# Filter layers spaced over more steps, the filter's output as split products, two norms' columns by transposes

## Chip, cores and metric

One core of a Trainium2 chip runs the kernel. The metric is the device time of one execution in microseconds (us). Engines: PE (TensorE matmul), DVE (VectorE), ACT (ScalarE), POOL (GpSimd, here mostly a queue of DMAs) and SP (the queue of the weight stream).

## What is computed

A backbone of two layers over 256 latent tokens of width 1024 (fp32), with 256 context tokens in layer 0:

```
for layer i in 0, 1:
  x = x + 0.5 * gate2 * rms(ffn(norm(x, shift0, scale1)))          # FFN 0 / FFN 2, ctx too in layer 0
  y = attention + short conv (layer 0)  |  Hyena long conv (layer 1)
  x = x + gate5 * rms(y)
  x = x + 0.5 * gate8 * rms(ffn(norm(x, shift6, scale7)))          # FFN 1 / FFN 3
norm(x, sh, sc) = rms(x) * g * (1 + sc) + sh
(gate, shift, scale)_b = (silu(c) @ w_mod[i] + b_mod[i])[b]        # nine blocks of 1024 per layer
filter: z (256 x 33); three times h = sin(freq * (h @ w + b)), width 64;
        filt = (h @ w4) (256 x 2048) * window; its spectrum is used by the long convolution of layer 1
```

## The kernel before

**Products.** fp32 operands are split into a high part (rounded to fp32r) and a low part (the rest): a product is three fp32r matmuls, high by high, high by low, low by high (L1671 to L1673, L1732 to L1734). The weights come as 350 units of 128 x 1024 through a ring of six buffers (SP, L463). A unit's high part is made on ACT (L617) and its low part on DVE (L1006), four units ahead of PE. Some small products are plain fp32 matmuls.

**The FFNs.** FFN 1 (second of layer 0), 2 and 3 run eleven turns of six steps; step (i, k) is turn i, unit k: steps 0 to 3 are gate and up columns (24 matmuls of 256 columns each), steps 4 and 5 the down product (12 matmuls of 512 each). Every engine has the same list of turns, and `peeled=at_steps(places, calls)` hangs further calls on steps of it; these places are written by hand for PE, ACT and DVE apart. There is no scheduler: each engine executes its list in order and waits on semaphores.

**Modulation jobs.** A job (layer, block, half, stream) is a product of c with 1024 x 512 of `w_mod`: POOL loads it in four chunks of 0.5 MB (`load_job`, L515) as DVE frees them, DVE makes eight multiply-adds (L1021, L1023) and a split (L1033), ACT the rounding (L694), PE two sums over the rows (`job_sum`, at the next turn's step 0). `JOBS` lists them by FFN, one for each turn; `JOB_0`, `JOB_L` are the first numbers. For gates (blocks 2, 5, 8) PE sums into `mean_p` and DVE makes the gate (`gate_out`, L1043 and L1045) in a tile that POOL filled with the bias (`load_gate`), times the gain of the norm in `z_tok` (`load_gain`, slot by `GATE_SLOT`). The other blocks' sums are gathered in `job_p`; after the last of a batch ACT copies them (`batch_rows`), PE turns them into columns (`batch_columns`) and DVE adds the bias (`batch_out`, `norm_coef`).

**The filter** runs beside FFN 1, at the steps `FILTER_AT`: three calls of `filter_layer` (PE, fp32, L2079, bank `mean_p`), each followed on DVE by `sine_argument` (seven dependent operations) and on ACT by `sine`, then four of `filter_out` (PE, fp32, L2089, banks `job_p` and `mean_p`), each followed on DVE by `filter_sums`. Weights, window and transform matrices come by POOL before FFN 1 (`filt_in`, L582 to L589).

**Norms 3 and 5** (`IN_PAIRS`: the latent and the context stream before the mixer of layer 0) have their transposed, scaled x made beside weight products: DVE makes a diagonal matrix of 1/rms (`spread`, L1114) and PE multiplies blocks of x by it (`norm_columns`, L1721), after the ninth context unit's down product (norm 3; its last two blocks after the thirteenth) and after the ninth unit of the input projection (norm 5). DVE and ACT then apply scale and shift.

**The opening of an FFN.** When the normed input is complete (`h_ready`) POOL orders the gate and gain loads of the coming gates, and after them the further chunks of jobs; at the same time SP's ring refills.

Of the kernel before, what the change touches and what calls it, by code (L numbers as in the profile page):

```python
# [22 lines left out]
F32 = mybir.dt.float32  # L23
# [52 lines left out]
        [(1, b, h, LAT) for b in (1, 3, 4, 2) for h in range(2)],  # L76
        [(1, b, h, LAT) for b in (6, 7, 5) for h in range(2)],
        [(1, 8, h, LAT) for h in range(2)]]
JOB_0 = [0, 22, 30, 36]
JOB_L = [AHEAD, 20, 28, 34]  # L80
# [10 lines left out]
GATE_SLOT = [0, 1, 0, 0, 0, 0]  # L91
# [111 lines left out]
def program(nc, wstream, wmod, cvec_in, bmod, gate_rows, small, x_in, ctx_in, rpb, mask_in, ident_in, turn_in, zfeat, fw1, fw2,  # L203
            fw3, fw4, fcols, window_in, dft_in, out):
    with ExitStack() as ctx:
# [115 lines left out]
        w4 = k_re[:, :, :].rearrange("p a b -> p (a b)")  # L321
        window = k_s
# [128 lines left out]
        odd_out = sem("odd_out")  # L451
        inv_done, inv_step = sem("inv_done"), sem("inv_step")
# [48 lines left out]
        def _(pool):  # L501
# [86 lines left out]
            pool.dma_start(w4[0:HY_FFN, :], fw4).then_inc(filt_in, 16)  # L588
            pool.dma_start(window, window_in).then_inc(filt_in, 16)  # L589
            pool.wait_ge(h_ready, 8 * 5)  # L590
            load_gate(1, 2)
            load_gain(1, 2)
# [3 lines left out]
            load_gate(1, 5)  # L596
            load_gain(1, 5)
# [12 lines left out]
        def _(a):  # L610
# [319 lines left out]

            def spectrum_out(i):
# [20 lines left out]
            ffn(1, peeled=at_steps([(6, 2)] + FILTER_AT, [lambda: batch_rows(1)] + [lambda l=l: sine(l) for l in range(3)]))  # L952
# [47 lines left out]
        def _(v):  # L1000
# [109 lines left out]
            def spread(q, t):  # L1110

                i = 2 * q + t
                reciprocal(q, t)
                nc.vector.tensor_scalar(diag[:, t, :], ident[:, :], rstd[:, i:i + 1], None, ALU.mult).then_inc(diag_done, 1)  # L1114
# [431 lines left out]
            def sine_argument(l):  # L1546

                if l == 0:
                    v.wait_ge(filt_in, 16 * 7)
# [12 lines left out]
                assert count[0] == FD_SIN[l]  # L1562

# [18 lines left out]
            ffn(1, peeled=at_steps([(7, 0)] + FILTER_AT, [lambda: (batch_out(1), norm_coef(9), norm_coef(11))]  # L1582
# [85 lines left out]
        def _(pe):  # L1668
# [45 lines left out]
            def norm_columns(q, t, kts=range(KT)):  # L1714
# [3 lines left out]
                for kt in kts:  # L1718
                    if q == 1 and t == 0 and kt % 2 == 0:
                        pe.wait_ge(xt_copied, kt // 2 + 1)  # L1720
                    ins = nc.tensor.matmul(columns_of(q, kt)[:, t * P:(t + 1) * P],  # L1721
                                           X[NORMS[q][2]][:, t, kt * P:(kt + 1) * P], diag[:, t, :], start=True, stop=True)
# [192 lines left out]
            for ft in range(FT):  # L1915
# [5 lines left out]
                if ft == 8:  # L1921
# [17 lines left out]
            for idx in range(16):  # L1939
# [8 lines left out]
                if idx == 8:  # L1948
                    norm_columns(5, 0)
                    norm_columns(5, 1)  # L1950
# [120 lines left out]
            def filter_layer(l):  # L2071
                if l == 0:
                    pe.wait_ge(filt_in, 16 * 7)
                    pe.wait_ge(gate_free, 10)
# [6 lines left out]
            def filter_out(i):  # L2081
                th, half = i % 2, i // 2
                if i == 0:
                    pe.wait_ge(fa, 3)
# [3 lines left out]
                for b, bank in enumerate((job_p, mean_p)):  # L2088
                    ins = nc.tensor.matmul(bank[:, :], hid[H, th * P:(th + 1) * P],  # L2089
# [261 lines left out]
```

## Time and profile before

| | us |
|---|---|
| median of 3 runs | 1338.75 (1336.57 to 1341.46) |
| profiled execution, its own time | 1343.3 |
| span of its profile | 1341.5 |
| PE busy | 1306.6 (97%) |
| DVE, ACT busy | 982.1 (73%), 632.9 (47%) |
| mean granted clock of PE | 0.992 of full |

The span is what the trace covers; the execution's own time has 1.8 us around it. Busy time of PE counts overlapping matmuls as modelled, so it shows where PE works, not how well; the start times of neighbouring matmuls tell the pace. A time in brackets in a timeline is the idle time before an instruction, with the one that released it.

### The profile page before, as it was taken

Reading aid. Unit: us, or ns where it says so; the run is one execution under the profiler, and the core shown is the slowest. Engines: PE = TensorE matmul, PEld = TensorE weight load, DVE = VectorE, ACT = ScalarE, POOL = GpSimd, SP = SyncE. Lnnn points to the kernel's source line nnn. Section 1 sums busy time; section 2 is a strip of 40 time slices with the busy share of each in tenths; the row PEclk is TensorE's granted clock in tenths of the full one; section 3 lists DMA queues with packets and bytes.
Section 4 is the critical chain, followed back from the end, with each engine's and each line's share of the span. In section 5 each row is a group of like instructions: output and inputs, shape, how many; then the busy total and the mean of one; then the engine's idle time right before and its main releaser. Section 6 shows DMA issues by size and latency. Waiting matters only on the chain.

```text
span 1341.5 us, 21469 instructions
## 1 busy us (share of the span) xinstructions
PE 1306.6 (97%) x7794; PEld 1125.8 (84%) x7794; DVE 982.1 (73%) x1447; ACT 632.9 (47%) x969; POOL 118.1 (9%) x209
## 2 busy tenths in 40 slices
PE   6899999999999999999999999999999999999997
PEld 3678777887778988789999868999998987989996
DVE  5788777788776776759888778887558797865554
ACT  6632333332376665755444337444447434644443
POOL 3000010111000422011111000110000000000000
PEclk8999999999999999999999989999999999999999
DMA  9555566777655753259888635886653536656652
GB/s 361 186 171 178 199 203 248 254 244 262 227 173 173 204 147 105 79 174 363 292 303 296 198 118 198 309 299 198 189 188 127 158 110 204 236 173 188 183 185 102
DMA packets 76359, 275.12 MB, mean 205 GB/s; under 512 B 9226, under 2 KB 9781, under 8 KB 75712
## 3 DMA queue, kind: packets, MB, share of 16 engines
q1 hardware_dynamic: 52128, 187.00, 42.4%
q0 software_dynamic: 24160, 87.12, 19.0%
q8 instruction: 50, 0.82, 0.2%
q14 instruction: 21, 0.17, 0.0%
HBM read 273.04 MB, written 1.05 MB: 204 GB/s over the span
## 4 chain that ended last, share of the span: by engine, by line
PE 86%; DVE 7%; ACT 3%; DMA 2%; issue 1%; DVEq 0%; SPq 0%; ACTq 0%
PE gu L1671 16%; PE gu L1673 16%; PE gu L1672 16%; PE acc L1732 8%; PE acc L1734 8%; PE acc L1733 8%; DVE wlo_r L1006 2%; PE acc L1721 2%; DMA wlo<-in_wstream_dram 1%; ACT whi L617 1%; PE acc L2017 1%; PE acc L2028 1%; DMA x_lat<-in_x_in_dram 1%; PE acc L1995 1%; PE acc L1996 1%
## 5 line engine op out<-in xcount | busy, mean ns | idle before, releaser
L1671 PE MATMUL gu<-h_hi,whi 128*128 128x256 f32 (+1 forms) x1688 | 518.0, 307 | 4.2 <-DVE h_lo L1131 1.3
L1672 PE MATMUL gu<-h_lo,whi 128*128 128x256 f32 (+1 forms) x1688 | 515.3, 305 | 0.0
L1673 PE MATMUL gu<-h_hi,wlo_r 128*128 128x256 f32 (+1 forms) x1688 | 515.0, 305 | 0.0
L1006 DVE TENSOR_TENSOR wlo_r<-wlo,whi 128x1024 fp32r<-128x1024 f32 x350 | 421.5, 1222 | 100.9 <-ACT whi L617 99.3
L617 ACT ACTIVATE whi<-wlo 128x1024 fp32r<-128x1024 f32 x350 | 360.3, 1049 | 97.8 <-DMA wlo<-in_wstream_dram 97.5
L1671 PEld LDWEIGHTS gu<-h_hi,whi 128*128 128x128 f32 x1688 | 318.8, 189 | 28.6 <-issue 4.0
L1672 PEld LDWEIGHTS gu<-h_lo,whi 128*128 128x128 f32 x1688 | 318.8, 189 | 19.0 <-issue 0.7
L1673 PEld LDWEIGHTS gu<-h_hi,wlo_r 128*128 128x128 f32 x1688 | 319.4, 189 | 15.5
L1023 DVE SCALAR_TENSOR_TENSOR part<-wm,cvec,part 128x512 f32<-128x512 f32 x266 | 199.5, 750 | 6.7
L1732 PE MATMUL acc<-whi,act_hi 128*128 128x512 f32 x440 | 176.7, 402 | 2.5 <-DVE act_lo L1219 2.0
L1734 PE MATMUL acc<-wlo_r,act_hi 128*128 128x512 f32 x440 | 174.9, 397 | 0.0
L1733 PE MATMUL acc<-whi,act_lo 128*128 128x512 f32 x440 | 174.5, 397 | 0.0
L515 POOL DMA_DIRECT2D wm<-in_wmod_dram x128 | 67.6, 529 | 734.0 <-DVE part L1023 459.1
L1732 PEld LDWEIGHTS acc<-whi,act_hi 128*128 128x128 f32 x440 | 83.2, 189 | 27.3 <-DVE act_lo L1219 3.9
L1734 PEld LDWEIGHTS acc<-wlo_r,act_hi 128*128 128x128 f32 x440 | 83.1, 189 | 20.0
L697 ACT ACTIVATE gated<-gu 128x256 f32<-128x256 f32 x66 | 25.3, 383 | 156.2 <-PE gu L1673 156.2
L1733 PEld LDWEIGHTS acc<-whi,act_lo 128*128 128x128 f32 x440 | 83.3, 189 | 17.8
L1214 DVE TENSOR_TENSOR act<-gated,gu 128x256 f32<-128x256 f32 x66 | 27.7, 420 | 80.2 <-ACT gated L697 79.9
L694 ACT ACTIVATE total_hi<-part 128x512 fp32r<-128x512 f32 x38 | 24.0, 631 | 78.6 <-DVE part L1023 78.6
L751 ACT ACTIVATE act_hi<-act 128x256 fp32r<-128x256 f32 x22 | 9.2, 419 | 103.6 <-DVE act L1304 103.6
L1219 DVE TENSOR_TENSOR act_lo<-act,act_hi 128x256 fp32r<-128x256 f32 x88 | 37.2, 423 | 20.4 <-ACT act_hi L701 16.4
L701 ACT ACTIVATE act_hi<-act 128x256 fp32r<-128x256 f32 x66 | 27.6, 418 | 44.2 <-DVE act L1214 44.2
(337 smaller groups left out, 1233.2 us busy)
## 6 DMA issues: line engine op xcount, KB each, us to landing
wlo<-in_wstream_dram SPq DMA_DIRECT2D x350, 512.0 KB, 3.6
wm<-in_wmod_dram POOLq DMA_DIRECT2D x132, 512.0 KB, 6.1
area<-in_wmod_dram POOLq DMA_DIRECT2D x11, 512.0 KB, 19.6
z<-in_gate_rows_dram POOLq DMA_DIRECT2D x6, 512.0 KB, 6.7
gate_keep<-in_gate_rows_dram POOLq DMA_DIRECT2D x5, 512.0 KB, 7.1
area<-in_rpb_dram POOLq DMA_DIRECT2D x32, 64.0 KB, 3.6
x_lat<-in_x_in_dram SPq DMA_DIRECT2D x1, 1024.0 KB, 7.5
area<-in_ctx_in_dram SPq DMA_DIRECT2D x1, 1024.0 KB, 8.8
```

The source lines that it names most:

```text
L515: pool.dma_start(wm[:, 2 * part_:2 * part_ + 2, :], src[:, 2 * part_:2 * part_ + 2, :]).then_inc(wm_landed[part_ // 2], 16)
L617: nc.scalar.activation(whi[:, phase % RING, :], raw[:, phase % RING, :], ACT.Copy).then_inc(hi_done, 1)
L1006: nc.vector.tensor_tensor(wlo[:, u.base % RING, :], raw[:, u.base % RING, :], whi[:, u.base % RING, :].bitcast(F32), ALU.subtract).then_in ...
L1023: ins = nc.vector.scalar_tensor_tensor(out=part[:, :], in0=wm[:, kt, :], scalar=c, in1=part[:, :], op0=ALU.mult, op1=ALU.add)
L1214: nc.vector.tensor_tensor(dst, gated[:, s, :], gu[:, s, T:2 * T], ALU.mult).then_inc(act_mul, 1)
L1219: nc.vector.tensor_tensor(act_lo[:, s, :], act[:, s, :], act_hi[:, s, :].bitcast(F32), ALU.subtract).then_inc(act_lo_done, 1)
L1671: nc.tensor.matmul(out_, w_hi, x_hi, start=start, stop=False, skip_group_check=True)
L1672: nc.tensor.matmul(out_, w_hi, x_lo, start=False, stop=False, skip_group_check=True)
L1673: return nc.tensor.matmul(out_, w_lo, x_hi, start=False, stop=stop, skip_group_check=True)
L1732: nc.tensor.matmul(y, x_hi[:, tok], whi[:, s, cols], start=kt_first, stop=False, skip_group_check=True)
L1733: nc.tensor.matmul(y, x_lo[:, tok], whi[:, s, cols], start=False, stop=False, skip_group_check=True)
L1734: ins = nc.tensor.matmul(y, x_hi[:, tok], wlo[:, s, cols], start=False, stop=kt_last, skip_group_check=True)
```

## The change

The two jobs of gate (1, 2) move from FFN 1 to FFN 2, the filter's calls take new steps, `w4` is loaded twice (rows 0 to 63 and 64 to 127) and rounded into `spare`, hid is put as high over low parts on 128 rows, so that one matmul of 128 rows makes hid_hi w_hi + hid_lo w_hi and a second of 64 rows adds hid_hi w_lo. For norms 3 and 5, DVE scales x itself into `spare` and PE transposes it. Norm 3's and norm 5's columns come one unit later. POOL no longer waits for `h_ready` ahead of FFN 1's jobs.

```diff
--- before.py
+++ after.py
@@ -73,11 +73,11 @@
 
 JOBS = [[(0, b, h, s) for b in (2, 3, 4) for h in range(2) for s in (LAT, CTX)]
         + [(l, b, h, LAT) for l, b in ((0, 5), (0, 8), (0, 6), (0, 7), (1, 0)) for h in range(2)],
-        [(1, b, h, LAT) for b in (1, 3, 4, 2) for h in range(2)],
-        [(1, b, h, LAT) for b in (6, 7, 5) for h in range(2)],
+        [(1, b, h, LAT) for b in (1, 3, 4) for h in range(2)],
+        [(1, b, h, LAT) for b in (6, 7, 2, 5) for h in range(2)],
         [(1, 8, h, LAT) for h in range(2)]]
-JOB_0 = [0, 22, 30, 36]
-JOB_L = [AHEAD, 20, 28, 34]
+JOB_0 = [0, 22, 28, 36]
+JOB_L = [AHEAD, 20, 26, 34]
 AHEAD_CHUNKS = 4 * AHEAD
 CHUNK_SLOT = [2, 3, 4, 5, 2, 3, 4, 5, 2, 3, None, 4, 5, None, 4, 5]
 AHEAD_LOADS = [(1, 0), (0, 0), (1, 1), (0, 1)]
@@ -88,7 +88,7 @@
 GATE_NORM = {2: 1, 5: 3, 8: 5}
 GATE_RES = {2: 0.5, 5: 1.0, 8: 0.5}
 GATE_JOBS = [job for jobs in JOBS for job in jobs if job[1] in GATE_NORM]
-GATE_SLOT = [0, 1, 0, 0, 0, 0]
+GATE_SLOT = [0, 1, 0, 0, 1, 0]
 
 
 COLS_AHEAD = [(0, b, h, s) for b, h in AHEAD_LOADS for s in (LAT, CTX)]
@@ -319,6 +319,10 @@
         p_f = y_f[:, 0:2, :]
         m_f = y_f[:, 2:4, :]
         w4 = k_re[:, :, :].rearrange("p a b -> p (a b)")
+        w4_lo = area_r[:, 0:2 * D]
+        w4_hi = spare_r[:, :, :].rearrange("p a b -> p (a b)")
+        hid_at = 10 * D + 7 * T
+        hid_both = area_r[:, hid_at:hid_at + T]
         window = k_s
         u_t = z
         u_f = spare[:, :, :].rearrange("p w (s n) -> p w s n", s=2)
@@ -449,6 +453,7 @@
         fp, fa, fd = sem("filter_pe"), sem("filter_act"), sem("filter_dve")
         tr_done, un_out, uf_done, yf_step = sem("tr_done"), sem("un_out"), sem("uf_done"), sem("yf_step")
         odd_out = sem("odd_out")
+        out_hi, out_lo = sem("out_hi"), sem("out_lo")
         inv_done, inv_step = sem("inv_done"), sem("inv_step")
         stored = sem("stored")
 
@@ -585,16 +590,15 @@
             pool.dma_start(fw[0:HY_FFN, 128:192], fw3).then_inc(filt_in, 16)
             pool.dma_start(fc[0:HY_FFN, :], fcols).then_inc(filt_in, 16)
             pool.dma_start(dft, dft_in).then_inc(dft_landed, 16)
-            pool.dma_start(w4[0:HY_FFN, :], fw4).then_inc(filt_in, 16)
+            for rows_ in (slice(0, HY_FFN), slice(HY_FFN, 2 * HY_FFN)):
+                pool.dma_start(w4[rows_, :], fw4).then_inc(filt_in, 16)
             pool.dma_start(window, window_in).then_inc(filt_in, 16)
-            pool.wait_ge(h_ready, 8 * 5)
-            load_gate(1, 2)
-            load_gain(1, 2)
             with pool.Fori(JOB_L[1] + 1, JOB_L[2] + 1) as l:
                 load_job(l, gemv, steps_before(l))
             pool.wait_ge(h_ready, 8 * 6)
-            load_gate(1, 5)
-            load_gain(1, 5)
+            for b in (2, 5):
+                load_gate(1, b)
+                load_gain(1, b)
             with pool.Fori(JOB_L[2] + 1, JOB_L[3]) as l:
                 load_job(l, gemv, steps_before(l))
 
@@ -928,6 +932,13 @@
                 a.wait_ge(fd, FD_SIN[l])
                 nc.scalar.activation(hid[0:HY_FFN, :], sin_r[0:HY_FFN, :], ACT.Sin).then_inc(fa, 1)
 
+            def output_his():
+                a.wait_ge(filt_in, 16 * 8)
+                for c in range(2):
+                    nc.scalar.activation(w4_hi[:, c * D:(c + 1) * D], w4[:, c * D:(c + 1) * D], ACT.Copy).then_inc(out_hi, 1)
+                a.wait_ge(fa, 3)
+                nc.scalar.activation(hid_both[0:HY_FFN, :], hid[0:HY_FFN, :], ACT.Copy).then_inc(out_hi, 1)
+
             def spectrum_out(i):
 
                 half, what, w = SPECTRUM[i]
@@ -949,7 +960,8 @@
                 spectrum_out(i + 2)
                 spectrum_out(i + 3)
 
-            ffn(1, peeled=at_steps([(6, 2)] + FILTER_AT, [lambda: batch_rows(1)] + [lambda l=l: sine(l) for l in range(3)]))
+            ffn(1, peeled=at_steps([(6, 4)] + SINE_AT + [(7, 5)], [lambda: batch_rows(1)]
+                                   + [lambda l=l: sine(l) for l in range(3)] + [output_his]))
             load_table(ACT.Sqrt)
             spectra_norms(8, U_FFN[2] + 2, 0)
             load_table(ACT.Silu)
@@ -1111,6 +1123,10 @@
 
                 i = 2 * q + t
                 reciprocal(q, t)
+                if q in IN_PAIRS:
+                    nc.vector.tensor_scalar(spare[:, t, :], X[NORMS[q][2]][:, t, :], rstd[:, i:i + 1], None,
+                                            ALU.mult).then_inc(diag_done, 1)
+                    return
                 nc.vector.tensor_scalar(diag[:, t, :], ident[:, :], rstd[:, i:i + 1], None, ALU.mult).then_inc(diag_done, 1)
 
             def scale_columns(q, kt):
@@ -1546,7 +1562,7 @@
             def sine_argument(l):
 
                 if l == 0:
-                    v.wait_ge(filt_in, 16 * 7)
+                    v.wait_ge(filt_in, 16 * 8)
                 v.wait_ge(fp, l + 1)
                 step(nc.vector.tensor_scalar(sin_a[H, :], mean_p[H, 0:T], fc[H, l:l + 1], fc[H, 3:4], ALU.add, ALU.mult))
                 settle()
@@ -1561,6 +1577,16 @@
                 step(nc.vector.tensor_scalar(sin_r[H, :], sin_a[H, :], PI_F, -PI_F, ALU.min, ALU.max))
                 assert count[0] == FD_SIN[l]
 
+            def output_los():
+                v.wait_ge(fa, 3)
+                for c in range(2):
+                    v.wait_ge(out_hi, c + 1)
+                    nc.vector.tensor_tensor(w4_lo[H, c * D:(c + 1) * D], w4[H, c * D:(c + 1) * D],
+                                            w4_hi[H, c * D:(c + 1) * D].bitcast(F32), ALU.subtract).then_inc(out_lo, 1)
+                v.wait_ge(out_hi, 3)
+                nc.vector.tensor_tensor(hid_both[HY_FFN:2 * HY_FFN, :], hid[H, :], hid_both[H, :].bitcast(F32),
+                                        ALU.subtract).then_inc(out_lo, 1)
+
             def filter_sums(i):
 
                 th, half = i % 2, i // 2
@@ -1579,7 +1605,7 @@
                                                     in1=p_f[:, th, cols], op0=ALU.mult, op1=ALU.add))
                 assert count[0] == FD_SUM[i]
 
-            ffn(1, peeled=at_steps([(7, 0)] + FILTER_AT, [lambda: (batch_out(1), norm_coef(9), norm_coef(11))]
+            ffn(1, peeled=at_steps([(7, 4), (8, 0)] + FILTER_AT, [lambda: (batch_out(1), norm_coef(9), norm_coef(11)), output_los]
                                    + [lambda l=l: sine_argument(l) for l in range(3)]
                                    + [lambda i=i: filter_sums(i) for i in range(4)]))
             norms(8, (U_FFN[2] + 2, U_FFN[2] + 3))
@@ -1718,8 +1744,12 @@
                 for kt in kts:
                     if q == 1 and t == 0 and kt % 2 == 0:
                         pe.wait_ge(xt_copied, kt // 2 + 1)
-                    ins = nc.tensor.matmul(columns_of(q, kt)[:, t * P:(t + 1) * P],
-                                           X[NORMS[q][2]][:, t, kt * P:(kt + 1) * P], diag[:, t, :], start=True, stop=True)
+                    if q in IN_PAIRS:
+                        ins = nc.tensor.transpose(columns_of(q, kt)[:, t * P:(t + 1) * P], spare[:, t, kt * P:(kt + 1) * P],
+                                                  ident[:, :])
+                    else:
+                        ins = nc.tensor.matmul(columns_of(q, kt)[:, t * P:(t + 1) * P],
+                                               X[NORMS[q][2]][:, t, kt * P:(kt + 1) * P], diag[:, t, :], start=True, stop=True)
                     if t == 1 and kt % 2:
                         ins.then_inc(hp_done, 1)
 
@@ -1918,7 +1948,7 @@
                     job_sum(len(JOBS[0]) - 1, JOBS[0][-1])
                 if ft == 3:
                     batch_columns(0)
-                if ft == 8:
+                if ft == 9:
                     pe.wait_ge(gate_free, 8)
                     norm_columns(3, 0, range(6))
                     norm_columns(3, 1, range(6))
@@ -1945,7 +1975,7 @@
                 if idx >= 6:
                     pe.wait_ge(proj_out, idx - 1)
                 column_unit(Unit(U_AB + idx), unit_bank(idx)[:, 0:T], lat)
-                if idx == 8:
+                if idx == 9:
                     norm_columns(5, 0)
                     norm_columns(5, 1)
 
@@ -2070,8 +2100,8 @@
 
             def filter_layer(l):
                 if l == 0:
-                    pe.wait_ge(filt_in, 16 * 7)
-                    pe.wait_ge(gate_free, 10)
+                    pe.wait_ge(filt_in, 16 * 8)
+                    pe.wait_ge(gate_free, 8)
                     w, x_ = fw[E, 0:64], zf[E, :]
                 else:
                     pe.wait_ge(fa, l)
@@ -2081,13 +2111,14 @@
             def filter_out(i):
                 th, half = i % 2, i // 2
                 if i == 0:
-                    pe.wait_ge(fa, 3)
+                    pe.wait_ge(out_lo, 3)
                     pe.wait_ge(mod_ready, AHEAD + 2)
                 else:
                     pe.wait_ge(fd, FD_READ[i - 1])
                 for b, bank in enumerate((job_p, mean_p)):
-                    ins = nc.tensor.matmul(bank[:, :], hid[H, th * P:(th + 1) * P],
-                                           w4[H, b * D + half * 512:b * D + half * 512 + 512], start=True, stop=True)
+                    times, cols = slice(th * P, (th + 1) * P), slice(b * D + half * 512, b * D + half * 512 + 512)
+                    nc.tensor.matmul(bank[:, :], hid_both[:, times], w4_hi[:, cols], start=True, stop=False)
+                    ins = nc.tensor.matmul(bank[:, :], hid_both[H, times], w4_lo[H, cols], start=False, stop=True)
                 ins.then_inc(fp, 1)
 
             def spectrum(i):
@@ -2099,7 +2130,7 @@
                                            start=(th == 0), stop=(th == 1))
                 ins.then_inc(fp, 1)
 
-            ffn(1, 4, peeled=at_steps([(6, 4)] + FILTER_AT, [lambda: batch_columns(1)]
+            ffn(1, 4, peeled=at_steps([(7, 0)] + FILTER_AT, [lambda: batch_columns(1)]
                                       + [lambda l=l: filter_layer(l) for l in range(3)]
                                       + [lambda i=i: filter_out(i) for i in range(4)]))
             pe.wait_ge(dft_landed, 16)
@@ -2214,7 +2245,8 @@
 SPECTRUM = [(half, what, w) for half in range(2) for what in ("re", "sine") for w in range(2)]
 
 ROWS_AT, BATCH_AT, COEF_AT = (4, 2), (4, 4), (5, 0)
-FILTER_AT = [(8, 3), (8, 5), (9, 1), (9, 3), (9, 5), (10, 1), (10, 3)]
+FILTER_AT = [(6, 2), (6, 5), (7, 2), (8, 4), (9, 0), (9, 4), (10, 0)]
+SINE_AT = [(6, 3), (7, 0), (7, 3)]
 
 
 def at_steps(places, calls):
```

## Rows read from the trace of the kernel before

**Rows 1.** The page: busy time, share of the span and instructions of each engine

```profile
PE 1306.6 (97%) x7794; PEld 1125.8 (84%) x7794; DVE 982.1 (73%) x1447; ACT 632.9 (47%) x969; POOL 118.1 (9%) x209
```

**Rows 2.** Waits of PE, 600 to 810 us: total us, times, longest us

```profile
PE job_p L2089 <- ACT area L929: 1.9, 1, 1.9
PE mean_p L2079 <- ACT area L929: 0.4, 1, 0.4
PE acc L1732 <- DVE act_lo L1219: 0.3, 1, 0.3
```

**Rows 3.** Timeline of PE: start us, us, engine line op, count, [idle <- releaser]

```profile
771.49 0.28 PE L1673 MATMUL gu<-h_hi,wlo_r 128*128 128x256 f32 x1
773.67 1.49 PE L2089 MATMUL job_p<-area 64*128 64x512 f32 x2 [1.90 <-ACT area L929]
...
776.79 0.79 PE L1732 MATMUL acc<-whi,act_hi 128*128 128x512 f32 x1
...
783.98 0.40 PE L1733 MATMUL acc<-whi,act_lo 128*128 128x512 f32 x1
784.22 0.40 PE L1734 MATMUL acc<-wlo_r,act_hi 128*128 128x512 f32 x1
...
786.46 0.38 PE L1671 MATMUL gu<-h_hi,whi 128*128 128x256 f32 x1
```

**Rows 4.** Stretches: busy us PE, PEld, DVE, ACT, POOL; granted PE clock, DMA share, GB/s

```profile
774.00:778.00 4.00, 4.00 (x7) 1.59 (x6) 2.40 (x4) 2.65 (x5) 0.00 (x0) 0.54 0.13 50
778.00:782.00 4.00, 4.00 (x13) 3.13 (x12) 3.77 (x6) 1.44 (x2) 0.00 (x0) 0.61 0.01 4
```

**Rows 5.** Timeline of PE around the columns of norm 5

```profile
464.12 0.28 PE L1673 MATMUL gu<-h_hi,wlo_r 128*128 128x256 f32 x1
464.24 3.75 PE L1721 MATMUL acc<-diag,area 128*128 128x128 f32 x32
467.74 0.37 PE L1671 MATMUL gu<-h_hi,whi 128*128 128x256 f32 x1
```

**Rows 6.** Timeline of ScalarE at the start of turn 8 of FFN 1

```profile
744.24 1.06 ACT L617 ACTIVATE whi<-wlo 128x1024 fp32r<-128x1024 f32 x1 [3.22 <-DMA wlo<-in_wstream_dram]
```

**Rows 7.** Groups of VectorE by form: count | busy us, mean ns | idle before us

```profile
L1006 DVE TENSOR_TENSOR wlo_r<-wlo,whi 128x1024 fp32r<-128x1024 f32 x350 | 421.5, 1222 | 100.9 <-ACT whi L617 99.3
...
L1043 DVE TENSOR_TENSOR gate_keep<-mean_p,gate_keep 128x512 f32<-128x512 f32 x10 | 6.8, 684 | 0.0
...
L1114 DVE TENSOR_SCALAR diag<-ident,rstd 128x128 f32<-128x128 f32 x16 | 4.6, 287 | 0.6
```

**Rows 8.** Timeline of PE around transposes of the attention (L2028)

```profile
538.70 0.29 PE L1974 MATMUL gu<-act_lo,turn_r 128*128 128x256 f32 x1
538.82 1.04 PE L2028 MATMUL acc<-ident,area 128*128 128x128 f32 x8
539.61 0.48 PE L1970 MATMUL job_p<-wm_r,area_r 128*128 128x512 f32 x1
```

**Rows 9.** Stretches at the openings of FFN 2 and FFN 3, columns as in rows 4

```profile
825.00:840.00 15.00, 15.00 (x104) 13.71 (x103) 13.59 (x20) 7.11 (x10) 1.59 (x3) 1.00 1.00 376
1175.00:1180.00 5.00, 3.30 (x15) 2.37 (x14) 4.96 (x8) 1.96 (x4) 0.00 (x0) 1.00 0.60 200
```

**Rows 10.** DMA queues, 604 to 626 us: packets, MB, share of 16 engines

```profile
q0 software_dynamic: 1025, 4.21, 51.1%
q1 hardware_dynamic: 1139, 4.17, 49.0%
```

**Rows 11.** Timeline of POOL: the first gate load, a chunk of the second job

```profile
821.64 0.53 POOL L544 DMA_DIRECT2D gate_keep<-in_gate_rows_dram  x1 [82.01 <-DVE h_lo L1131]
...
828.24 0.53 POOL L515 DMA_DIRECT2D wm<-in_wmod_dram  x1 [3.32 <-DVE part L1023]
```

**Rows 12.** Timeline of VectorE: where that job is first used

```profile
838.99 0.48 DVE L1021 TENSOR_SCALAR part<-wm,cvec 128x512 f32<-128x512 f32 x1
```

**Rows 13.** The stretch with these transposes, columns as in rows 4

```profile
538.00:545.00 7.00, 6.97 (x44) 5.63 (x43) 5.88 (x14) 7.00 (x17) 0.00 (x0) 1.00 0.19 75
```

## The prediction

> **What bounds the kernel.** I read the page first: TensorE (PE) is busy 97% of the span [rows 1], so what counts is what PE executes and the few places where it stands. The list of PE's waits in the second half of layer 0 has one large entry: the first product of the filter's output waits 1.9 us for the last sine, and a filter layer waits 0.4 us for an earlier one [rows 2]. The timeline of PE shows the place: the matmul before starts at 771.49, the filter's product at 773.67 and the next weight matmul at 776.79 [rows 3]. The table of stretches shows what the stall leaves behind: for 8 us the granted clock is 0.54 and 0.61 of full, about the lower level of 1.2 GHz instead of 2.4 [rows 4]. So this wait costs more than its own length. The profiled execution took 1343.3 us (span 1341.5), 4.6 us more than the median of 1338.75 and outside the three runs; I take differences within its trace and set them against the median.
>
> **Filter products, PE.** Each `filter_out` is two fp32 calls of 512 columns, and an fp32 call is two instructions. A split matmul of 512 columns follows its neighbour by 0.24 us (783.98 to 784.22), so a group without a wait lasts from 784.46 to 786.46: 2.0 us [rows 3]. The change issues four split matmuls, at 0.24 us each 0.96 us. That is the lower bound; the upper is 2.0, if the alternation of 128 and 64 rows breaks the pipelining. The rows of the same number format are the nearest, so I take 1.0. Four groups: 4 x (2.0 - 1.0) = 4.0 us saved, all on the path.
>
> **The stall and its clock.** From 771.61 (771.49 plus the 0.12 by which a 256-column matmul is followed, 464.12 to 464.24 [rows 5]) to 776.79 are 5.2 us where 2.0 are work: 3.2 us. The 24 weight matmuls from 776.79 to 784.46 take 7.7 us instead of 24 x 0.24 = 5.8: 1.9 us. Together 5.1 us; with the wait of 0.4 [rows 2] 5.5 us. They go if the chain of sines is ready in time. The layers move from two steps apart (8,3), (8,5), (9,1) to three and three steps, and the first product comes eight steps behind the last layer, so the stall of 5.1 has a whole turn of PE work as cover. Next late is what the change adds: ScalarE's two 1024-wide roundings at (7,5), about 1.05 us each, and one of 256. A stretch in which ScalarE stood idle for 3.22 us waiting for a weight unit lies just there [rows 6]. VectorE then makes two subtractions of 1.22 us [rows 7] and a short one at (8,0), against five steps until PE wants them. Were that cover gone they would cost their own 2 x 1.05 + 2 x 1.22 = 4.5 us and the two short ones. The wait for the eighth filter DMA costs nothing: it is ordered a whole FFN earlier; POOL issues one DMA more and the queue carries 0.5 MB more, but without the two gate loads (1.0 MB) at that place. PE's only wait in that opening was 0.3 [rows 2], so this is worth nothing to 0.3; I take nothing.
>
> **Columns of norms 3 and 5.** The matmul against the diagonal is fp32 with 128 columns: 32 instructions for one norm last from 464.24 to 467.74, 3.5 us [rows 5]. A transpose of fp32 is one instruction per call: in the attention eight calls are eight instructions and last from 538.82 to 539.61, 0.79 us [rows 8]. Sixteen make 1.6 us, so 1.9 saved per norm, 3.8 for both; the lower bound is nothing, if a transpose from `spare` ran twice as the matmul does. VectorE's `spread` grows from 0.29 us to something between that and the 1.22 of a 1024-wide operation of two inputs [rows 7], at most 0.9 us, four times. It hides behind PE's weight matmuls, and the transposes are put one unit later, which gives it more cover (2.8 us of column or down matmuls). Behind it on VectorE is the split of a unit wanted four units on. Cost nothing; without this cover 3.7 us.
>
> **The moved gate jobs.** Both jobs of block 2 go from turns 6 and 7 of FFN 1 to turns 4 and 5 of FFN 2, with their eight multiply-adds, one rounding, two sums on PE, and a gate output of two operations of about 0.7 us [rows 7]; block 5 follows in turns 6 and 7. PE's work is only moved. VectorE runs the same turns it ran before, four with a gate output in a row; each turn has its own idle time, so I charge nothing. What changes is the start of FFN 2: POOL orders four loads there in place of two, 1.05 MB more, ahead of the second job's chunks. At that time the DMA engines are full at 376 GB/s [rows 9]. In the opening of FFN 1 the two queues moved 4.21 and 4.17 MB, so they share evenly [rows 10], and POOL's has 188 GB/s: 2.8 us a load. The first gate load is ordered at 821.64 and the second chunk of the job at 828.24 [rows 11], now the sixth load in line: 821.64 + 6 x 2.8 = 838.4 against a first use at 838.99 [rows 12]. It is just in time. At the same point FFN 3, whose opening has two gate loads, lets PE stand for 1.7 us in 5 [rows 9]. Bounds 0 and 1.7; I take 0.5 as nearer to the opening of FFN 2 itself, where PE is busy throughout.
>
> **Sum.** 4.0 + 5.5 + 3.8 - 0.5 = 12.8 us, taken from the median: 1325.9 us.
>
> **Rivals.**
> - *The loads at FFN 2 become the stall.* One chunk late by a few us stops VectorE, the next activation's low part is late, PE stands over 2 us and its clock falls as in [rows 4]. Price as measured, 5.1 instead of 0.5: 1330.5 us. For it: a computed margin of 0.6 us. Against: the queues start before the weights press.
> - *The filter's wait only moves.* ScalarE waits for VectorE inside its own order, and the added roundings could make PE wait once at the first product. The 5.5 us are not won: 1331.4 us. Against: five to eight steps of cover.
> - *Transposes lower the clock.* Transposes in a row would count as no work, and the clock would be halved after each of the three bursts (norm 3 in two parts, norm 5). One low stretch cost 4 x 0.46 + 4 x 0.39 = 3.4 us [rows 4], three 10.2: 1336.2 us. Against: the stretch with the attention's transposes has clock 1.00 [rows 13], though there in bursts of eight. The Trainium skill, "TensorE: Matmul & The Clock Gate", section "PE-mode transpose", says that the full clock does not engage in transpose mode because it does not count as PE being busy in the same way. By that rule this case would be the likely one; the row speaks against it.
> - *The transpose saves no instruction* (two passes after all): 3.8 less, 1329.8 us. Against: [rows 8].
> - *Slower.* The backlog of POOL's queue at FFN 2 does not drain: each turn orders four more chunks behind the gate loads, and VectorE is late in turns 1 to 4. Each such wait has the price of the stall seen, 5.1. From the third on (15.3 over 12.8 + 0.5) the gain is gone; four make 20.4 and 1345.9 us. Against: in FFN 3 the backlog is over by 1175, with 200 GB/s and a DMA share of 0.60 [rows 9].
>
> **How the numbers follow.** Forecast 0.70; loads at FFN 2 0.11; the wait moves 0.07; clock after transposes 0.05; two passes 0.03; slower 0.04. A measurement here tells 0.3%, 4.0 us. Faster by more (below 1334.7): 0.70 + 0.11 + 0.07 + 0.03 = 0.91. Within: 0.05. Slower: 0.04. The forecast with its bounds (opening 0 to 1.7, groups 0.96 to 1.3, the median's own scatter of some 2.5 us) is 1322 to 1330; the range reaches from 1321 to 1332 to take in the two next rivals.
>
> **What would show it.** Right: no wait of PE for a sine or for `out_lo` above 0.3 us; no stretch of FFN 1 with a clock below 1; from the last weight matmul before a filter group to the next about 1 us instead of 2; 16 transposes in some 1.6 us with clock 1.00 behind them; VectorE not waiting for `wm` in turn 1 of FFN 2. Wrong: idle PE between 820 and 850 us, a dip of the clock after norm 3 or 5, two instructions per transpose, or filter matmuls spaced by more than 0.3 us.

## The result and the profile after

The kernel after takes 1331.12 us (median of 15 runs, 1328.84 to 1336.24), beside 1339.48 for the kernel before (15 runs, 1336.57 to 1343.46): ratio 0.9947, interval 0.9936 to 0.9958. By the medians that is 8.4 us less; the ratio, which goes by all runs, makes it 7.1 (5.6 to 8.6). The terms below are set against the medians. Forecast were 1325.9 us, 12.8 less. The profiled execution took 1331.64 us (span 1330.0). Its mean granted clock is 0.997, that of the profiled execution of before was 0.992.

Busy time by engine in the page of after, beside [rows 1]:

```profile
PE 1294.5 (97%) x7762; PEld 1116.5 (84%) x7762; DVE 985.9 (74%) x1450; ACT 636.0 (48%) x972; POOL 118.5 (9%) x210
```

The waits of PE from 600 to 1010 us in after (the filter beside FFN 1, and FFN 2), beside [rows 2]:

```profile
PE acc L1762 <- DVE act_lo L1235: 1.8, 2, 1.5
PE job_p L1726 <- DVE total_lo L1045: 1.0, 1, 1.0
```

No wait for a sine is left. The longest entry is new, and it lies in the opening of FFN 2. Three stretches of after (columns as in [rows 4]): the filter's second half with its outputs, the opening of FFN 2 and that of FFN 3.

```profile
738.00:800.00 62.00, 62.00 (x385) 51.61 (x384) 44.36 (x61) 29.44 (x46) 0.00 (x0) 1.00 0.50 153
...
825.00:840.00 15.00, 13.51 (x91) 12.09 (x90) 13.44 (x20) 8.38 (x12) 2.11 (x4) 1.00 0.87 296
...
1160.00:1170.00 10.00, 8.04 (x45) 6.61 (x44) 9.82 (x14) 5.17 (x8) 0.00 (x0) 1.00 0.53 157
```

PE stands nowhere from 738 to 800 and the clock is full, where [rows 4] had 0.54 and 0.61. From 825 to 840 it is 1.5 us short of full, where [rows 9] had 15.00 of 15.

**Where the time went.** Both traces have the same sequence of weight products, so their turns can be laid side by side; a figure is how much later (+) or earlier (-) the same weight product starts in after, less what was so at the end of the stage before. For later use the columns hold experiments too, each against the profiled execution of before.

| stage | after | e1 | e10 | e3 | e4 | e5 | e6 | e7 | e8 |
|---|---|---|---|---|---|---|---|---|---|
| start to first down product | -3.4 | -3.3 | -3.7 | -3.6 | -3.8 | +0.2 | +0.3 | -3.2 | -5.4 |
| to the input projection (norm 3) | -1.9 | -1.7 | -1.9 | 0.0 | -1.8 | 0.0 | -1.8 | -1.7 | -1.7 |
| to FFN 1's first down (norm 5) | -2.3 | -2.3 | -2.3 | -0.2 | -2.7 | -0.3 | -2.4 | -2.1 | -3.0 |
| FFN 1, turns 6 to 10 (filter) | -8.3 | -11.5 | -8.3 | -6.7 | 0.0 | -4.4 | -6.7 | -11.5 | -11.5 |
| FFN 2, opening | +2.9 | +3.9 | 0.0 | +2.3 | 0.0 | 0.0 | +2.3 | 0.0 | 0.0 |
| FFN 2, rest | +1.2 | +1.4 | +1.2 | +1.3 | 0.0 | 0.0 | +1.1 | +1.6 | +1.3 |
| FFN 3, opening | +0.2 | -0.4 | +2.0 | +0.4 | -0.2 | -0.3 | 0.0 | +0.1 | -0.8 |

e9, the kernel after once more, has -3.7, -1.9, -2.3, -8.3, +2.8, +1.2 and -0.5 in these lines, e2 has -5.3, -1.8, -2.2, -8.3, 0.0, +1.3 and +1.0. Turns 0 to 5 of FFN 1 and what lies behind FFN 3's opening differ by 0.8 us at most. The first line of after is no work of the change. Stretches of the start-up, 24 to 48 us, of before, after and e6:

```profile
24.00:48.00 24.00, 21.17 (x106) 15.41 (x107) 17.88 (x28) 16.71 (x26) 1.05 (x2) 0.79 0.73 285
```
```profile
24.00:48.00 24.00, 21.48 (x124) 14.19 (x125) 19.00 (x31) 17.55 (x27) 1.05 (x2) 0.93 0.84 321
```
```profile
24.00:48.00 24.00, 20.79 (x103) 15.17 (x104) 17.95 (x29) 16.78 (x25) 0.80 (x2) 0.79 0.74 285
```

e6 shares the start-up with after and has the clock of before here, 0.79, and its lateness. e4 and e5 have before's program there, and one is 3.8 us early at a clock of 1.00, the other 0.2 late at 0.79: one kernel's executions differ in it. Without this line after's stages give -8.2, and the medians differ by 8.4.

### The profile page after: what moved, and what is told of

It is laid out like the page before. It is cut to its first block, busy times and chain, and to the rows that moved or that the text cites. A ratio compares the mean times of both kernels' runs of the same rounds, so it can differ in the third digit from the quotient of the medians.

```text
span 1330.0 us, 21413 instructions
## 1 busy us (share of the span) xinstructions
PE 1294.5 (97%) x7762; PEld 1116.5 (84%) x7762; DVE 985.9 (74%) x1450; ACT 636.0 (48%) x972; POOL 118.5 (9%) x210
## 4 chain that ended last, share of the span: by engine, by line
PE 83%; DVE 9%; ACT 4%; DMA 3%; issue 1%; DVEq 0%; SPq 0%; ACTq 0%
PE gu L1697 16%; PE gu L1699 16%; PE gu L1698 15%; PE acc L1762 8%; PE acc L1764 8%; PE acc L1763 8%; DVE wlo_r L1018 3%; DMA wlo<-in_wstream_dram 2%; PE acc L1751 2%; ACT whi L621 1%; PE acc L2047 1%; PE acc L2058 1%; DMA x_lat<-in_x_in_dram 1%; PE acc L2025 1%; PE acc L2026 1%
```

## The experiments

All are compared with before on the same chip; the medians of before there were 1338.75 (e1 to e4, 23 runs), 1339.21 (e5 to e8, 17 runs) and 1339.42 (e9, e10, 12 runs). Theory A grew with the readings of after: groups of 1.6 us in place of 1.0, and an opening of FFN 2 held up by gate loads in POOL's queue, which slow the weight stream.

**e1: the second product on 128 rows too.** In after the four split matmuls of a group start at 748.23 to 749.41 and the next weight matmul at 749.84 (timeline of PE in after):

```profile
748.00 0.40 PE L1764 MATMUL acc<-wlo_r,act_hi 128*128 128x512 f32 x1
748.23 0.40 PE L2120 MATMUL job_p<-spare_r,area_r 128*128 128x512 f32 x1
748.56 0.49 PE L2121 MATMUL job_p<-area_r 64*128 64x512 f32 x1
748.98 0.50 PE L2120 MATMUL mean_p<-spare_r,area_r 128*128 128x512 f32 x1
749.41 0.50 PE L2121 MATMUL mean_p<-area_r 64*128 64x512 f32 x1
749.84 0.50 PE L1762 MATMUL acc<-whi,act_hi 128*128 128x512 f32 x1
750.18 0.40 PE L1763 MATMUL acc<-whi,act_lo 128*128 128x512 f32 x1
```

Weight matmuls follow each other by 0.23; the group takes 1.61 and gives another 0.11 to the weight matmul behind it (0.34). e1 adds hid_lo times w_lo, which costs no further instruction:

```diff
-  tensor_tensor(w4_lo[H, c*D:(c+1)*D], w4[H, ...], w4_hi[H, ...].bitcast(F32), ALU.subtract)
+  tensor_tensor(w4_lo[:, c*D:(c+1)*D], w4[:, ...], w4_hi[:, ...].bitcast(F32), ALU.subtract)
-  ins = matmul(bank[:, :], hid_both[H, times], w4_lo[H, cols], start=False, stop=True)
+  ins = matmul(bank[:, :], hid_both[:, times], w4_lo[:, cols], start=False, stop=True)
```

> The changed kernel, with the low parts of w4 made on all 128 rows and the second product of filter_out also on 128 rows (it adds the term hid_lo w_lo). Theory A, the alternation of 128 and 64 rows slows the split products: the four matmuls of a group follow each other by 0.24 us instead of 0.33, 0.42, 0.43 and 0.43, a group takes about 1.0 us instead of 1.6, and the kernel is 4 x 0.6 = 2.4 us faster than the changed one (some 10 us faster than the kernel before). Rival: the pace of 0.43 comes from something else in these matmuls (their operands, their banks); then the group still takes 1.6 us and the time is that of the changed kernel (some 8 us faster than before).

Measured: 1329.30 us (6 runs, 1326.64 to 1330.94), ratio 0.9926 (0.9905 to 0.9947). The same group in the timeline of PE in e1:

```profile
748.54 0.40 PE L1764 MATMUL acc<-wlo_r,act_hi 128*128 128x512 f32 x1
748.77 0.40 PE L2120 MATMUL job_p<-spare_r,area_r 128*128 128x512 f32 x1
749.01 0.39 PE L2121 MATMUL job_p<-area_r 128*128 128x512 f32 x1
749.23 0.39 PE L2120 MATMUL mean_p<-spare_r,area_r 128*128 128x512 f32 x1
749.46 0.39 PE L2121 MATMUL mean_p<-area_r 128*128 128x512 f32 x1
749.69 0.39 PE L1762 MATMUL acc<-whi,act_hi 128*128 128x512 f32 x1
749.92 0.39 PE L1763 MATMUL acc<-whi,act_lo 128*128 128x512 f32 x1
```

The group takes 0.92 and nothing behind it is late: 0.80 less a group, 3.2 for four, as the stage shows (-11.5 against -8.3). So a change between 128 and 64 rows costs about 0.2 us, four times a group: 0.1 in the step ahead of the changed matmul (0.33 for 0.23) and 0.1 in the step behind (0.34); in between, where both meet, the steps are 0.42 and 0.43. That the change costs, and not the 64-row matmul as such, is settled at e6. The opening of FFN 2 lost 1 us more: from 832 to 840 its granted clock was 0.79. The median gained 1.8 of the 3.2, with intervals that overlap.

**e2 and e10: the gate loads behind the second and third job of FFN 2.** One kernel, run twice. Its new loop loads jobs 27 and 28 whole, eight chunks of 0.5 MB: in e10 the first gate load is ordered at 836.14, behind the eighth chunk at 835.53. Where the texts below say "the second job's first two chunks", it is these eight.

```diff
             pool.wait_ge(h_ready, 8 * 6)
+            with pool.Fori(JOB_L[2] + 1, JOB_L[2] + 3) as l:
+                load_job(l, gemv, steps_before(l))
             for b in (2, 5):
                 load_gate(1, b)
                 load_gain(1, b)
-            with pool.Fori(JOB_L[2] + 1, JOB_L[3]) as l:
+            with pool.Fori(JOB_L[2] + 3, JOB_L[3]) as l:
```

> The changed kernel, with the four loads of gate rows and gains of blocks 2 and 5 ordered after the second and third job of FFN 2 (numbers 27 and 28) instead of ahead of them. Theory A, these loads delay the weight stream: the waits of PE of 1.0 us (total_lo) and 1.5 us (act_lo) in turns 0 and 1 of FFN 2 go, the opening is 2.9 us shorter, 11 us faster than before. Rival: the opening suffers from something else (PE arrives there earlier, the ring is less full) and the waits stay above 1.5 us in sum; the time is that of the changed kernel, 8 us faster than before.

Measured: 1330.93 us (6 runs, 1327.83 to 1333.42), ratio 0.9942 (0.9922 to 0.9963). The opening's loss is gone in the trace, the median is after's and not the 11 us under before of theory A. So it was run again, beside after:

> The kernel after once more, beside e10 on one chip, so that both share the runs of before. Every theory: 1331.1 us within 1, 8 us under before. In the trace the start-up is either as slow as before's, e5's and e6's (first down matmul within 0.3 us of 75.3) or 3 to 5 us faster: theory A says that it is chance and both are possible, rival B that the change itself shortens it (then it is faster here again).

> e2's kernel once more: after with block 2's and 5's gate loads behind the second job's first two chunks. Theory A (the trace is right, e2's median was scatter of six runs): 1.5 to 3 us under e9, since the opening of FFN 2 gives 2.9 us and FFN 3's takes up to 1.0. Rival B (the traces' gain does not reach the median): within 0.7 us of e9.

Measured: e9 1330.66 (7 runs, 1329.19 to 1336.79), ratio 0.9945 (0.9926 to 0.9964); e10 1330.52 (6 runs, 1328.67 to 1331.86), ratio 0.9934 (0.9917 to 0.9952). Rival B for e10. What holds PE up in after's FFN 2 are late weight units. Timeline of ACT in after (the unit's rounding, and in brackets what it waited for):

```profile
820.06 1.06 ACT L621 ACTIVATE whi<-wlo 128x1024 fp32r<-128x1024 f32 x1 [3.04 <-DMA wlo<-in_wstream_dram]
...
822.62 1.06 ACT L621 ACTIVATE whi<-wlo 128x1024 fp32r<-128x1024 f32 x1 [0.98 <-DMA wlo<-in_wstream_dram]
825.18 1.06 ACT L621 ACTIVATE whi<-wlo 128x1024 fp32r<-128x1024 f32 x1 [1.50 <-DMA wlo<-in_wstream_dram]
827.71 1.06 ACT L621 ACTIVATE whi<-wlo 128x1024 fp32r<-128x1024 f32 x1 [1.47 <-DMA wlo<-in_wstream_dram]
```

Four units in a row wait for their DMA, 7.0 us together, 2.55 us apart. In that time POOL's queue moves the four gate loads and four chunks ordered from 805.69 to 817.66 (timeline of POOL in after):

```profile
805.69 0.53 POOL L549 DMA_DIRECT2D gate_keep<-in_gate_rows_dram  x1 [110.35 <-DVE h_lo L1147]
...
807.25 0.53 POOL L555 DMA_DIRECT2D z<-in_gate_rows_dram  x1
808.44 0.53 POOL L520 DMA_DIRECT2D wm<-in_wmod_dram  x1 [0.66 <-DVE part L1035]
```

Queues of after from 805 to 827 us, as [rows 10]:

```profile
q0 software_dynamic: 1151, 4.19, 53.5%
q1 hardware_dynamic: 933, 3.42, 38.7%
```

The weight stream (q1) gets 3.42 MB while POOL's has 4.19; in e10 it was 3.66 beside 2.24 over the same stretch. A weight unit ordered there takes 10.2 us to land in after, 5.5 in e10 (medians of eight). VectorE, behind the late roundings, gets its subtractions and the job's multiply-adds close together, and the activation's low part comes late (timelines of DVE and of PE in after):

```profile
827.41 0.48 DVE L1033 TENSOR_SCALAR part<-wm,cvec 128x512 f32<-128x512 f32 x1
...
831.27 1.60 DVE L1035 SCALAR_TENSOR_TENSOR part<-wm,cvec,part 128x512 f32<-128x512 f32 x2
832.79 2.35 DVE L1018 TENSOR_TENSOR wlo_r<-wlo,whi 128x1024 fp32r<-128x1024 f32 x2
...
836.06 0.42 DVE L1235 TENSOR_TENSOR act_lo<-act,act_hi 128x256 fp32r<-128x256 f32 x1
```
```profile
836.53 0.50 PE L1762 MATMUL acc<-whi,act_hi 128*128 128x512 f32 x1 [1.49 <-DVE act_lo L1235]
```

In e10 the opening of FFN 2 has no such wait. That of FFN 3 has one in every trace, in e10 longer than in after and with a lower clock (timeline of PE and a stretch of e10):

```profile
1164.28 0.50 PE L1764 MATMUL acc<-whi,act_hi 128*128 128x512 f32 x1 [2.28 <-DVE act_lo L1237]
```
```profile
1160.00:1170.00 10.00, 7.72 (x32) 6.04 (x31) 9.96 (x13) 4.84 (x6) 0.00 (x0) 0.83 0.37 109
```

So the repaired opening wins 2.9 us, and in these two traces the next one gives back 2.0 and 1.0. The stage there is the length of this wait against before's 1.70: 2.75 in e2 at clock 1.00 makes its +1.0; e10's 2.28 makes 0.6, and the other 1.4 go with its clock of 0.83. But the wait was 1.96 in after and 1.26 in e9, which are one kernel, and 1.78 in e7, which has e10's gate loads. Whether the later gate loads lengthen it, or executions differ so, was not isolated; nor do the medians show e2's and e10's gain.

**e3: only the places.** After with fp32 products and diagonal norms, these back at their old units; the filter's places and the moved gate jobs stay.

```diff
-  matmul(bank, hid_both[:, times], w4_hi[:, cols]); matmul(bank, hid_both[H, times], w4_lo[H, cols])
+  matmul(bank[:, :], hid[H, th*P:(th+1)*P], w4[H, b*D + half*512 : ... + 512], start=True, stop=True)
-  if q in IN_PAIRS: tensor_scalar(spare[:, t, :], X[...][:, t, :], rstd, None, ALU.mult); return
-  if q in IN_PAIRS: transpose(columns_of(q, kt)[...], spare[:, t, kt*P:(kt+1)*P], ident)
```

> The changed kernel with fp32 products and with the columns of norms 3 and 5 by the diagonal again: what is left is the new places of the filter's calls, the moved gate jobs and the gate loads. Theory A: the wait of 1.9 us for the last sine and the low clock behind it go (5.5 us by the trace), the opening of FFN 2 costs 2.9, so 2.6 us faster than before. Rival: the low clock behind the wait belongs to the profiled execution more than to the usual one; then only the wait itself is won, 2.3 us, and the time is within 1 us of the kernel before, or slower.

Measured: 1335.49 us (12 runs, 1332.49 to 1339.91), ratio 0.9973 (0.9958 to 0.9988): 3.3 under before. Theory A's 2.6 is the nearer; the rival's 1 or less lies outside the interval (1.6 to 5.6).

**e4: only the transposes.** Before with the two hunks of norms 3 and 5 and their later places.

```diff
+  if q in IN_PAIRS: tensor_scalar(spare[:, t, :], X[NORMS[q][2]][:, t, :], rstd[:, i:i + 1], None, ALU.mult)
+  if q in IN_PAIRS: transpose(columns_of(q, kt)[:, t*P:(t+1)*P], spare[:, t, kt*P:(kt+1)*P], ident[:, :])
-  if ft == 8:   (norm 3)      -  if idx == 8:   (norm 5)
+  if ft == 9:                 +  if idx == 9:
```

> The kernel before with the columns of norms 3 and 5 by a scaled copy and transposes alone. Theory A: 1.8 us a norm, 3.7 us faster than before, clock 1.00 behind the transposes. Rival: VectorE's longer spread or the later columns give some of it back, 1.5 to 2.5 us faster only; or the clock falls and it is slower.

Measured: 1335.64 us (12 runs, 1334.06 to 1341.07), ratio 0.9979 (0.9964 to 0.9994): 3.1 under before. The interval, 0.8 to 4.8 us, holds theory A's 3.7 and the rival's 1.5 to 2.5; the stages, -1.8 and -2.7, speak for theory A. Norm 5 in the timeline of PE in after, beside [rows 5]:

```profile
462.85 0.28 PE L1699 MATMUL gu<-h_hi,wlo_r 128*128 128x256 f32 x1
462.96 1.91 PE L1748 MATMUL acc<-ident,spare 128*128 128x128 f32 x16
464.63 0.36 PE L1697 MATMUL gu<-h_hi,whi 128*128 128x256 f32 x1
```

Sixteen instructions in 1.67 us, where 32 took 3.5. The clock stays (stretch of after):

```profile
464.00:474.00 10.00, 10.00 (x88) 10.00 (x86) 7.92 (x14) 5.60 (x11) 0.00 (x0) 1.00 0.47 159
```

e4 keeps the wait for the sine, 1.9 and 0.4 us, and the dip behind it; its stretch:

```profile
768.00:776.00 8.00, 8.00 (x25) 5.91 (x24) 6.99 (x9) 3.03 (x4) 0.00 (x0) 0.70 0.17 43
```

**e5: only the filter's outputs later,** in the kernel before.

```diff
-FILTER_AT = [(8, 3), (8, 5), (9, 1), (9, 3), (9, 5), (10, 1), (10, 3)]
+FILTER_AT = [(8, 3), (8, 5), (9, 1), (9, 4), (10, 0), (10, 2), (10, 3)]
```

> The kernel before, with the four filter outputs and the last layer's successors alone spread out: layers at (8,3), (8,5), (9,1) as before, outputs at (9,4), (10,0), (10,2), (10,3) in place of (9,3), (9,5), (10,1), (10,3). Nothing else differs: fp32 products, diagonal norms, gate jobs in their old turns. Theory A (the first output stands 1.9 us for the last sine, and the low clock behind it costs about as much again): the stall is gone, clock 1.00 behind it, FFN 1's second half 3.2 to 5.1 us shorter in the trace, median 2.1 to 5.1 us under before. Rival B (the clock's dip belongs to slow executions, and fast ones have the stall alone): median 1 to 2 us under before. Rival C (the stall only moves to a later output, because VectorE's sums come one behind the other): no gain, 0 to 1 us.

Measured: 1335.04 us (12 runs, 1332.28 to 1339.28), ratio 0.9962 (0.9948 to 0.9976): 4.2 under before. Where the stall was, timeline of PE in e5:

```profile
774.02 0.40 PE L1734 MATMUL acc<-wlo_r,act_hi 128*128 128x512 f32 x1
774.35 1.12 PE L2089 MATMUL job_p<-area 64*128 64x512 f32 x2
775.31 1.02 PE L2089 MATMUL mean_p<-area 64*128 64x512 f32 x2
776.97 0.50 PE L1732 MATMUL acc<-whi,act_hi 128*128 128x512 f32 x1 [0.64 <-DVE act_lo L1219]
```

and its stretches there, beside [rows 4]:

```profile
774.00:778.00 4.00, 3.36 (x10) 1.53 (x9) 2.54 (x4) 2.65 (x5) 0.00 (x0) 1.00 0.48 188
778.00:782.00 4.00, 4.00 (x28) 3.62 (x27) 3.80 (x6) 2.25 (x3) 0.00 (x0) 1.00 0.20 41
```

The stage is 4.4 us shorter, with 0.64 and the layer's 0.4 still standing: 5.4 in all. Stall and clock cost what theory A says, also outside the trace: rival B's 1 to 2 us lie outside the interval (3.2 to 7.0).

**e6: after with fp32 products.** The product lines as in e3; no second load of `w4`, no roundings, no subtractions.

> The kernel after with the outputs as fp32 products again (no split weights, no second load of them, no roundings at (7,5)); transposes, places and moved gate jobs as in after. Theory A (four split matmuls take 1.6 us a group, fp32 2.0): 4 x 0.4 = 1.6 us slower than after, 6.7 us under before. Rival B (the split product also brings or costs something beside PE, in VectorE's subtractions or the 0.5 MB more of weights): off by over 1.5 us from that, on either side. By the prediction's own term it would be 4.0 us slower than after.

Measured: 1332.67 us (6 runs, 1328.99 to 1335.59), ratio 0.9943 (0.9922 to 0.9964). A group in the timeline of PE in e6:

```profile
751.17 0.40 PE L1763 MATMUL acc<-wlo_r,act_hi 128*128 128x512 f32 x1
751.50 1.12 PE L2118 MATMUL job_p<-area 64*128 64x512 f32 x2
752.46 1.02 PE L2118 MATMUL mean_p<-area 64*128 64x512 f32 x2
753.41 0.49 PE L1761 MATMUL acc<-whi,act_hi 128*128 128x512 f32 x1
753.75 0.39 PE L1762 MATMUL acc<-whi,act_lo 128*128 128x512 f32 x1
```

From the matmul ahead to the second one behind are 2.58 us, in after (748.00 to 750.18) 2.18, in e1 (748.54 to 749.92) 1.38. 0.40 x 4 = 1.6, the difference of the stages (-6.7 against -8.3) and about that of the medians (1332.67 against 1331.12), whose intervals overlap. The split as built brought 1.6 us.

This group also tells a change of rows from a 64-row matmul. In before, fp32 products of 128 rows stand behind a weight product (timeline of PE in before):

```profile
807.49 0.40 PE L1734 MATMUL acc<-wlo_r,act_hi 128*128 128x512 f32 x1
807.72 3.60 PE L2098 MATMUL gu<-area 128*128 128x512 f32 x8
811.16 1.88 PE L2098 MATMUL job_p<-area 128*128 128x512 f32 x4
```

The first follows by the usual 0.23, so the other number format costs nothing; eight take 3.44, 0.43 each. Four instructions of 64 rows in e6 take 1.91 (751.50 to 753.41), 0.19 over four times 0.43, and the weight steps on both sides (0.33, 0.34) are 0.1 too long each. That is 0.4 for two changes, though four matmuls have 64 rows; after has 0.8 for four changes, with two. The cost goes by the changes.

**e7: e1's and e10's edits together. e8: also block 8's gate load one place earlier.**

```diff
             pool.wait_ge(inv_done, KT)
+            load_gate(1, 8)
             load_job(JOB_L[3])
             pool.wait_ge(h_ready, 8 * 8)
-            load_gate(1, 8)
```

> The kernel after with the second product on 128 rows too (low weights twice, as e1) and block 2's and 5's gate loads of layer 1 behind the second job's first two chunks (as e2). Theory A (the parts add: 3.2 us for even rows and 2.9 us of FFN 2's opening, less 1 given back at FFN 3's): 3 to 5 us under after, about 1326 to 1328. Rival B (e2's gain is not there in the median because it is given back at FFN 3's opening and in the start-up; even rows alone count): about e1, 1329.3, that is 1.8 us under after.

> As e7, and block 8's gate load of layer 1 is ordered one place earlier, ahead of the first chunk of the last stage's job, so that FFN 3 opens with one load less. Theory A (FFN 3's opening is held up by what POOL's queue orders there, as FFN 2's was): PE's idle time behind 1150 us smaller by about 1 us, total 0.5 to 1.5 us under e7. Rival B (the weight stream of FFN 3's opening is as late without it): same as e7 within 0.5 us, or the load only disturbs the end of FFN 2, 0 to 1 us slower.

Measured: e7 1325.55 us (6 runs, 1324.42 to 1329.10), ratio 0.9900 (0.9880 to 0.9920); e8 1323.97 (6 runs, 1321.97 to 1328.74), ratio 0.9896 (0.9875 to 0.9917). PE's wait in FFN 3's opening, in e7 and in e8:

```profile
1161.13 0.50 PE L1764 MATMUL acc<-whi,act_hi 128*128 128x512 f32 x1 [1.78 <-DVE act_lo L1237]
```
```profile
1156.73 0.50 PE L1764 MATMUL acc<-whi,act_hi 128*128 128x512 f32 x1 [0.93 <-DVE act_lo L1237]
```

e7's median is 5.6 us under after's, a little more than theory A's 3 to 5, and beats both kernels (the intervals, 0.9880 to 0.9920 and after's 0.9936 to 0.9958, do not touch). In e7's trace FFN 3's opening took nothing back (+0.1, where e10 had +2.0), and the parts added; that even rows are the reason isn't shown. In e8 the wait is half as long and the stage 0.9 shorter; the median is 1.6 lower than e7's, but the intervals overlap, and the two executions of after differ by 0.7 in this stage, those of e2 and e10 by 1.0. e8's gain is not shown.

## Why the prediction was right or wrong

The direction and its main cause were right; the size was 4.4 us too large (12.8 against 8.4, or against 7.1 by the ratio of all runs). 1331.12 lies inside the range only because that was widened from 1330 to 1332 for two rivals, neither of which occurred: that is luck. Two of the signs that it named for being wrong came: idle PE between 820 and 850 us, and filter matmuls more than 0.3 us apart. By its own terms:

| term | predicted | measured |
|---|---|---|
| filter products | 4.0 | 1.6 (e6 against after) |
| stall, its clock, layer wait | 5.5 | 5.4 (e5: 4.4 and the 1.0 it kept) |
| columns of norms 3 and 5 | 3.8 | 4.2 (1.9 and 2.3); e4's median 3.1 |
| opening of FFN 2 | -0.5 | -2.9 |
| sum | 12.8 | 8.3 |

- **Filter products: the step that failed.** It took 0.24 us for each split matmul, "the rows of the same number format are the nearest", and left the alternation of 128 and 64 rows to the upper bound. That bound was the mechanism: four changes of rows cost 0.8 us a group. With even rows (e1) a group does take 0.92, the predicted 0.96. The trace of before had a hint: its fp32 groups of 64 rows stand between weight matmuls of 128, and the first starts at 784.54, 0.33 behind the matmul at 784.22 [rows 3], where the prediction had put it at 784.46. The term was 2.4 too large.
- **Opening of FFN 2: right place, wrong queue, wrong size.** The prediction followed POOL's queue and asked whether the sixth load lands before its use at 838.99 [rows 11, 12]. In after that job's first multiply-add waits for nothing, while the weight units that share the engines with those loads are late. Evenly shared engines [rows 10] mean that what one queue orders delays the other; the step asked only one of them. What it put at 0.5 cost 2.9. Its upper bound of 1.7 was too low, having come from another opening. The rival of the late loads foresaw the chain from VectorE to the activation's low part, but began it with a late chunk instead of late weight units; its 5.1 was too high, since the clock did not fall in after; in e1 it did (0.79).
- **Stall and clock.** 5.5 predicted, 5.4 found. The dip is also in e4's trace, and e5's median confirms the price outside of traces. The covers held: no wait for `out_lo`, no PE wait from ScalarE's two roundings at (7, 5). e3's stage (-6.7) holds the 5.4 and 1.2 of work moved to FFN 2's rest, where it is back as +1.3. "PE's work is only moved" holds.
- **Columns.** Sixteen transposes in 1.67 us against 1.6 predicted, one instruction each. VectorE's scaling takes 0.75 us against 0.29, hidden. So 1.8 of norm 5's 2.3 are the transposes; e3 and e5, which have none, show -0.2 and -0.3 in this stage, and about 0.2 is left without account.
- **Rivals.** The filter's wait did not move. The transposes did not lower the clock: 1.00 in the stretch behind norm 5 above, and 1.00 from 398 to 410, where norm 3's end. The Trainium skill, "TensorE: Matmul & The Clock Gate", section "PE-mode transpose", says that the full clock does not engage in transposes; by that rule norm 5's stretch would have been lower, and after would have been near the 1336.2 of the rival. The trace speaks against it here, for bursts of 16 between weight products. No backlog of POOL's queue held FFN 2's later turns (+1.2 is moved work), so the slower case did not occur.
- **The reference execution.** The prediction took differences inside a trace that was 4.6 us over its median. 3.4 us of that lie in the start-up, with the lower clock at 24 to 48 us, far from the change, and did not enter the sum.

## What to carry to other kernels

Price a matmul with the neighbours it will have: between 128-row products a 128-row one costs 0.23 us and a 64-row one about 0.6 (an estimate: two of each took 1.72), so fill the free rows, here even with a term that isn't needed. When one queue gets more to load, look for the harm in the other queue that shares the DMA engines, above all where the weight stream refills. A gain in one opening may not reach the end (e10's trace lost 2.0 of 2.9 in the next), so read every opening of the new trace before counting it.

## What the runs showed of the hardware that was not expected

- A change between 64 and 128 rows: about 0.2 us each, from 1.72 against 0.92 us for a group with four changes and one with none (after and e1), at full clock. In e6 two changes cost 0.4 with four matmuls of 64 rows.
- Executions of one kernel differ by their mean granted clock: e9's had 1329.19 to 1331.96 us at 0.997 to 0.999 and 1336.79 at 0.993. The traces show one place, the start-up, 24 to 48 us: 0.79 in before, e5 and e6, 0.93 in after, e3, e7 and e10, 1.00 in e1, e2, e4, e8 and e9, which is after once more. This scatter is as large as most single edits here, and it is why traces laid side by side settled what medians of six runs could not.
- Waits of PE of like length did and did not bring the clock down: behind 1.90 us before the filter's product it was 0.54 [rows 2, 4], while the stretch of after with a wait of 1.96 us in FFN 3's opening has 1.00 (1160 to 1170 above); 2.05 us in e1's FFN 2 opening came with 0.79, 2.28 in e10's FFN 3 opening with 0.83, and 2.75 in e2's there with 1.00. The length of the wait alone does not tell it.
